# Squared-ReLU MLP, up projection: order of ScalarE's and VectorE's work at a change of token group

## The reference

```python
x = layer_norm(DEEPNORM_ALPHA * x + heads @ w_out, ln_mix_g, ln_mix_b)
h = jnp.square(jax.nn.relu(x @ w_ff1))                                   # 1024 -> 4096
x = layer_norm(DEEPNORM_ALPHA * x + h @ w_ff2, ln_ffn_g, ln_ffn_b)
```

## Time and profile before

| | |
|---|---|
| median of 3 runs | 2436.46 us (2435.9 to 2437.45) |
| profiled execution, its own time | 2437.59 us |
| profiled execution, span | 2435.9 us |
| TensorE busy with matmuls | 2364.5 us (97% of the span) |
| VectorE busy | 1578.0 us (65%) |
| ScalarE busy | 1087.0 us (45%) |
| mean granted TensorE clock | 0.99 |
| stretch of `mlp_up` on TensorE | 866.6 to about 1657 us |

### The profile page before, as it was taken

How to read it: one execution, slowest core, us unless ns; L and a number is a source line. 1 busy time by engine, 2 the same in 40 slices (tenths; PEclk the granted TensorE clock), 3 DMA queues, 4 the chain that set the end, 5 groups by cost and what they waited for, 6 DMA issues and landing times. The chain is left out here.

```text
span 2435.9 us, 34771 instructions
## 1 busy us (share of the span) xinstructions
PE 2364.5 (97%) x12004; PEld 2063.9 (85%) x12004; DVE 1578.0 (65%) x2222; ACT 1087.0 (45%) x1782; POOL 182.0 (7%) x245
## 2 busy tenths in 40 slices
PE   6999999999999979999999999999999999999997
PEld 5888887999788779999999788888888888888886
DVE  8655376766666677786666655556566866764658
ACT  3111146888211155565555544445444444443331
POOL 1000001211223200000000000000000100000002
PEclk9999999999999989999999999999999999999999
DMA  7766776322456666677677655558877887787662
GB/s 263 294 255 232 283 217 218 81 69 86 133 198 238 257 252 233 245 278 279 230 256 269 270 216 195 201 198 301 283 225 213 269 298 226 211 284 248 196 192 104
DMA packets 220464, 547.85 MB, mean 225 GB/s; under 512 B 21688, under 2 KB 90936, under 8 KB 200764
## 3 DMA queue, kind: packets, MB, share of 16 engines
q1 hardware_dynamic: 204272, 488.19, 57.5%
q0 software_dynamic: 16080, 58.20, 7.4%
HBM read 365.95 MB, written 180.36 MB: 224 GB/s over the span
## 5 line engine op out<-in xcount | busy, mean ns | idle before, releaser
L71 PE MATMUL e_bank<-e_hi,e_lo 128*128 128x512 f32 x1120 | 435.8, 389 | 0.1
L73 PE MATMUL e_bank<-e_hi 128*128 128x512 f32 x1120 | 435.7, 389 | 0.0
L72 PE MATMUL e_bank<-e_lo,e_hi 128*128 128x512 f32 x1120 | 435.7, 389 | 0.0
L71 PE MATMUL u_bank<-u_x_hi,u_wa_lo 128*128 128x384 f32 (+1 forms) x768 | 272.7, 355 | 6.8 <-ACT c_vt_raw L1940 3.4
L2206 DVE TENSOR_TENSOR e_lo<-e_raw,e_hi 128x896 fp32r<-128x896 f32 (+1 forms) x168 | 189.9, 1135 | 126.0 <-ACT e_hi L2177 125.7
L73 PE MATMUL u_bank<-u_x_hi,u_wa_hi 128*128 128x384 f32 (+1 forms) x768 | 271.3, 353 | 0.0
L2177 ACT CAST e_hi<-e_raw 128x896 fp32r<-128x896 f32 (+1 forms) x168 | 165.2, 984 | 209.9 <-PE e_bank L73 199.7
L71 PEld LDWEIGHTS e_bank<-e_hi,e_lo 128*128 128x128 f32 x1120 | 210.2, 188 | 44.7 <-DVE e_lo L2206 1.0
L73 PEld LDWEIGHTS e_bank<-e_hi 128*128 128x128 f32 x1120 | 210.2, 188 | 43.7
L72 PEld LDWEIGHTS e_bank<-e_lo,e_hi 128*128 128x128 f32 x1120 | 210.2, 188 | 43.5
L71 PE MATMUL u_bank<-u_x_hi,u_wb_lo 128*128 128x384 f32 (+1 forms) x576 | 203.9, 354 | 6.4 <-DVE u_x_first L1786 4.9
(11 more groups left out here) (279 smaller groups left out, 4615.5 us busy)
## 6 DMA issues: line engine op xcount, KB each, us to landing
u_w_sum<-s_ws SPq DMA_DIRECT2D x34, 1024.0 KB, 4.8
c_vt_raw<-w_ff SPq DMA_DIRECT2D x24, 1024.0 KB, 6.8
c_q_raw<-w_ff SPq DMA_DIRECT2D x24, 1024.0 KB, 6.8
s_h<-c_k_raw SPq DMA_DIRECT2D x32, 768.0 KB, 6.7
e_raw<-s_t SPq DMA_DIRECT2D x96, 256.0 KB, 3.7
e_raw<-s_h SPq DMA_DIRECT2D x112, 192.0 KB, 2.9
ab_place<-w_ff SPq DMA_DIRECT2D x18, 1024.0 KB, 8.4
s_h<-c_k_raw SPq DMA_DIRECT2D x96, 192.0 KB, 2.5
```

The lines of the kernel that those rows point to most:

```text
L71: tensor.matmul(out, w_lo, m_hi, start=first, stop=False, skip_group_check=again)
L72: tensor.matmul(out, w_hi, m_lo, start=False, stop=False, skip_group_check=again)
L73: return tensor.matmul(out, w_hi, m_hi, start=False, stop=last, skip_group_check=again)
```

## The change

It touches only the steps on both sides of a change of group, and no instruction is added or removed.

- ScalarE, last step of group 0: `x_high(1, 4)` moves ahead of the finish of quarter 22. Last step of both groups: the finish of quarter 21 leaves this step and stands in the next one, behind the copy of the first product. So `wb_high`, the third part of the weights, and that copy stand earlier in the order.
- ScalarE, second change: `x_high(2, 3)` too moves from the last step to the next one, behind the copy.
- VectorE, first change: `x_low(1, 6)` moves ahead of `h_sums`, from its place behind c22 to the one behind `x_low(1, 5)`.
- VectorE, second change: `x_low(2, 3)` moves from ahead of `wb_low` to behind u2, and `h_sums` from ahead of `wa_low_raw` to behind `x_low(2, 6)`.

```diff
 VectorE, body(g, p, s, start, end)
-                elif start:
-                    x_low(g, 5 - g)
+                elif start and g == 1:
+                    x_low(g, 4)
                 wb_low(n, s)
...
                 if start:
+                    if g == 2:
+                        x_low(g, 3)
                     if g != 1:
                         x_low(g, 4)
                     x_low(g, 5)
-                if not start or g:
+                    if g == 1:
+                        x_low(g, 6)
+                if (not start or g) and not (start and g == 2):
                     h_sums(n - 1, UP_GROUPS[g - 1 if start else g][1])
...
-                if start:
+                if start and g != 1:
                     x_low(g, 6)
                     if g == 0:
                         wa_low_raw(n + 1, 1 - s)
+                    else:
+                        h_sums(n - 1, UP_GROUPS[g - 1][1])
 ScalarE, body(g, p, s, start, end)
                 if start:
                     if g:
-
-                        finish(n - 1, 12, u2[:, 0:UP_GROUPS[g - 1][1]], UP_GROUPS[g - 1][1])
+                        before = UP_GROUPS[g - 1][1]
+                        if g == 2:
+                            x_high(g, 3)
+                        finish(n - 1, 21, u3[:, 0:before], before)
+                        finish(n - 1, 12, u2[:, 0:before], before)
...
                 if near == 1:
                     x_high(g + 1, 3 - g)
+                    if g == 0:
+                        x_high(g + 1, 4)
                 finish(n, 22, c22[:, 0:w], w)
-                if near == 1:
-                    x_high(g + 1, 4 - g)
-                finish(n, 21, u3[:, 0:w], w)
+                if near != 1:
+                    finish(n, 21, u3[:, 0:w], w)
```

## The result

The changed kernel takes 2439.51 us (median of 20 runs, 2437.47 to 2442.46), the kernel before 2436.36 us (20 runs, 2432.37 to 2439.24). I had forecast +1.5 us, in a range from 2433.8 to 2440.6 us.

The account below looks back on a forecast made before the run. TensorE, busy 2364.5 of 2435.9 us, was taken as the bound, so only its waits or clock cost time. Terms +0.97 + 0.9 - 0.33 = +1.5 us took the median from 2436.46 to 2438.0 us, range 2433.8 to 2440.6 us.

Parts of the forecast that it names:

- The frame: Up projection, both changes of group: TensorE's waits sum to 8.3 us; with the clock at most about 10 us to gain.
- First change, c22: Before P3, the wait is only renamed from slot 6 to c22; with the later start it becomes 2.7 us.
- First change, slot 4: ScalarE idles 1.0 us for slot 4's load, so VectorE's slot 5 and P3 start later: +0.97 us.
- First change, clock: Behind P3's wait of 2.7 us the clock may fall: +0.9 us taken, between 0 and +1.7 us.
- Second change, waits: No wait before P2, 1.4 us before P5, 3.5 us before P3, which starts earlier: -0.33 us.
- Second change, transfers: Loads of weights issued earlier on SP's queue leave slot 6's landing unmoved: 0, with a bound of 3.0 us.
- Rival (d): Second change: earlier loads of weights take bandwidth from slot 6, so slower, at its bound +5.3 us, 2441.8 us; chance 0.07.
- the same fall of the clock as now: Second change, behind P3's wait of 3.5 us: a fall as before, worth 1.7 us, hiding P3's later end.

Follow-up runs that it names:

- low6_only: The kernel before with only VectorE's rest of slot 6 moved ahead of the sums of h at the first change; 2436.98 us, ratio 1.0000.
- slot4_behind_22: The changed kernel with the cast of slot 4 back behind the finish of 22; 2437.13 us, ratio 1.0001 against the kernel before.
- after_again: The changed kernel unchanged, timed and profiled a second time; 2438.75 us, ratio 1.0009 against the kernel before.
- first_only: The changed kernel with the edits at the second change of group undone; 2439.09 us, ratio 1.0011 against the kernel before.
- second_only: The changed kernel with the edits at the first change of group undone; 2436.33 us, ratio 0.9997 against the kernel before.
- sums_in_idle: The changed kernel with VectorE reordered (sums of h into idle time, c22 before the weights' rest) and slot 4's cast behind the finish of 22; 2434.66 us, ratio 0.9985.
- sums_in_idle_busy: The kernel of sums_in_idle with 6 further unused matmuls ahead of P3's wait in the first step of group 2; 2431.90 us, ratio 0.9979.

## Why the prediction came out as it did

**The frame.** The change moves only waits of the up projection, and not by their whole 8.3 us. Right: 8.3 us became 8.6, in part under other names.

**First change, c22.** Right and shown. P3 needs slot 6 and c22, and the same VectorE work stands ahead of the later of the two, whichever it is. low6_only is this step alone: 16.08 us against 16.07.

**First change, slot 4.** Right in kind, its size was too large: +0.97 us forecast, +0.49, +0.69 and +0.41 us measured in the three profiles with the edit and without further matmuls, +0.53 us between the two kernels with them. The load took 11.7 us again (issued at 1095.83, cast at 1107.51), but ScalarE itself came to it later: its cast of the sums of weights began at 1104.18, 8.35 us behind that issue, and before at 1105.69, 7.76 us behind. So it idled 0.5 us and not 1.0. slot4_behind_22 shows that this edit is the cause, since the stretch is then 15.98 us. P2's wait did not stay at 1.26 us as forecast: it is 0.86.

**First change, clock.** I took +0.9 us between 0 and 1.7, since 2.7 us of wait lay halfway between one that kept the clock and one that lost it. (No row of the prediction shows the clock behind the 1.75 us; the trace has it at 1.00 from 1120 to 1135 us.) That waits of the same length are followed by a fall in one execution and not in another was not in the prediction. Three of the four profiles with a wait of 2.6 us and no matmuls in it show a fall, and one of the three with 1.65 to 1.8 us. With 1.6 us a fall this is 1.2 less 0.5, +0.7 us, an estimate from seven profiles. That it is near the +0.9 us is luck: a half between two bounds was put in for want of a reason.

**Second change, waits.** Right. Forecast were none before P2, 1.4 before P5, 3.5 before P3, and P3 0.33 us earlier. Measured were none, 1.6 and 3.4 us. From P1 to P3 it took 21.87 and 21.82 us in the changed kernel and 22.13 before; over the profiles without further matmuls the mean is 21.95 us with these edits (4) and 22.11 us without (3), with a spread of 0.8 us among the latter. I can't tell more than that it is small.

**Second change, transfers.** Right: 0 of a bound of 3.0 us, since slot 6 landed 14.02 us behind P1, and 13.96 before. SP's loads went out at 1352.24, 6.95 us behind that P1 where it was 9.21, so 2.3 us earlier (forecast 2.7). Yet the sums of weights landed 16.3 us behind that P1 and 15.7 us before. Rival (d) is out. The rule of the Trainium skill ("DMA: Bandwidth & Descriptors", Queues, rings and completion order), one queue in ring order, gives the same 0; the landings agree with it here, and no trace shows the order of the packets.

**The step that was mis-sized** is "the same fall of the clock as now" at the second change. I took one fall of 1.7 us for both kernels. The three profiles with the old edits there show 3.4, 0 and 3.4 us at the low clock, and the four with the new ones 3.4, 6.8, 6.8 and 3.4. From P3 to the last product matmul the three take 289.28 us in the mean and the four 290.27, +1.0 us (a fall counts for less in the new order: that of after_again began 1.4 us before P3, in the wait itself). Together with the first change the term is +1.7 us and not +0.9. The new sum is +0.5 - 0.2 + 1.7 = +2.0 us; measured are +3.2 (1.7 to 4.6) and, in after_again, +2.2 us (0 to 4.4).

**What stays open.** How much of the loss is the clock's, and how its part divides. The profiles put the larger part of it at the second change (+1.0 and +0.7 us), while the times put the whole loss at the first (first_only +2.7 us, second_only -0.7 us, each with 2.2 us either way). Seven profiles are too few for a share of falls. The 0.45 us in group 0 come with the wait for `wa_low_sum` ahead of P1 of group 1, which follows that later cast, and the cast waits for its load (4.31 us, and 3.73 before). P1's wait is 0.3 to 0.8 us in the profiles with edits. It is also 0.36 us in that of low6_only and 0.66 us in that of second_only, whose steps there are those of before; it is not told apart from chance.

**sums_in_idle** fell short of its 7 us at both changes. At the first, 2.05 us came back up to P3, but 0.6 us were lost in the products behind it (221.20 us to the next group and not 220.6), for a cause that no run isolates. At the second the clock fell for 6.8 us, and it was forecast to stay up; sums_in_idle_busy shows that price, 2.85 us. The wait was longer too. I put slot 6 of the second change at what its landing allows, some 2 us of wait. But slot 5 was late too, so the sums began at 1359.17 and slot 6 at 1362.77, 1.8 us after its cast was done at 1361.0, and the wait was 2.8 us. VectorE's lines there:

```profile
1359.17 0.55 DVE L1824 TENSOR_TENSOR c_k_raw<-c_k_raw 128x384 f32<-128x384 f32 x1
...
1362.77 2.28 DVE L1786 TENSOR_TENSOR u_x_first<-u_x_first,u_x_hi 128x2048 fp32r<-128x2048 f32 x1
```

## What to carry to other kernels

When a wait names one operand, list all that the waiting instruction needs and sum the work ahead of each on its own engine: if the same work stands ahead of two of them, changing their order only renames the wait. A gain comes from filling time in which the engine idles for something else, as the sums of h did. Behind a TensorE wait (here 1.8 to 3.8 us) price a fall of the clock as well, as a chance and not as a certainty; where the wait can't be removed, some matmuls in it whose result nobody reads can be worth more than a new order.

## What was not expected of the hardware

The falls of the clock are no fixed property of a wait. Behind 2.64 us it fell in one execution and not in another of the same kernel. Behind 1.77 us it fell once, and behind 3.17 us once it did not. Where it fell it was low for 3.4 us, or for 6.8 us behind waits of 3.46, 3.78 and 2.81 us. The first cost 1.6 us, the second 2.85 us where it can be read off. In the four profiles with further matmuls ahead of P3 it fell at neither change, though P3 started no earlier: at the second change 0.5 to 1.6 us of idle time in one piece were left. Two of the four have such matmuls at the first change too, with 0.4 and 1.3 us left; the other two wait only 0.4 us there by their order of work.
